# A router product with its weight columns stationary and the tokens streamed

## The chip, the cores and the metric

The kernel runs on one core of one Trainium2 chip. The metric is the device time of one execution, in microseconds (us), lower is better. The times are those of whole executions; the profile is of one execution of its own.

## The reference

One decoder layer in float32: 1024 tokens of width 1024. A mixer (a gated convolution, and stick-breaking attention in 8 heads) is followed by the output projection and the residual sum, and then by a hierarchical mixture of experts. The change is about the router, the first lines of `hierarchical_moe`:

```
xf = rms_norm(x)                               # 1024 tokens x 1024
g_logits = xf @ w_group  + b_group             # 4 columns
e_logits = xf @ w_expert + b_expert            # 32 columns
g_idx = argmax(g_logits)                       # one of 4 groups per token
e_in_group = e_logits.reshape(N, 4, 8)[g_idx]  # its 8 experts
top_v, top_i = top_k(e_in_group, 2)            # two experts per token
```

Each token is then multiplied with the three weight matrices of its two experts, weighed by its gates and added to the residual.

## The kernel before, in words

The kernel is a row of blocks with a barrier of all engines between them: projections, attention and convolution; then the block at line 807, in which the change lies; then the choice of experts (line 1032); then the loop over the 32 experts, the blocks that didn't fit, and the sum.

The block at line 807 goes over eight tiles of 128 tokens, m = 0 to 7. TensorE has an order written out by hand (lines 862 to 885). `multiply(m, h, ...)` forms one half (512 columns) of the output projection of a tile in 24 products: fp32 is split into a high and a low part, both fp32r, and three products (lines 840 to 842) of stationary 128x128 and streamed 128x512 make one of the eight steps. VectorE adds the residual (`add`, line 934), ScalarE squares and sums (909, 911), and VectorE scales the row with the norm (936, 938). TensorE turns the normalised tile in eight transposes (`turn`, line 851), ScalarE copies it out as `xn2T` (line 901), and TensorE forms the router logits of that tile (`route`, line 859). VectorE adds the bias (`bias`, line 942). GpSimd and VectorE prepare the high and low parts of the next tiles (832, 922).

TensorE's queue for tile m is: the first half of the projection of m, `turn(m - 1)`, the second half of m, `route(m - 1)`. VectorE's queue is `add(m)`, the low part of tile m + 2, `bias(m - 1)`. After the loop come `turn(7)`, `route(7)` and `bias(7)`, and then the barrier.

The router product of a tile is eight products of plain fp32, each of which the chip runs as two passes (16 weight loads and 16 matmuls). The stationary operand is the turned tile (128 rows by 128 tokens) and the streamed one `router_w[:, k]` (36 columns); the result is `ps[:, 6 + m % 2, 0:36]`, tokens on partitions. `router_b` holds the bias broadcast to all 128 partitions; it is loaded in two transfers (lines 323, 324) in the first block, on SyncE's queue between loads of x tiles (line 308).

Other lines that are spoken of: 407 is the input projection (128x128 stationary, 512 streamed, fp32r). In attention, 443 to 445 are the scores (64 rows by 128 columns stationary), 446 adds the mask (128x128), 456 transposes, and 466 multiplies with the values (128 rows by 64 columns stationary, 128 streamed, plain fp32).

Of the kernel before, what the change touches and what calls it, by code (L numbers as in the profile page):

```python
# [19 lines left out]
ALU = mybir.AluOpType  # L20
# [3 lines left out]
P = 128  # L24
# [19 lines left out]
def hymba_moe_layer(nc, x, norm_mix_w, w_in, conv_w, q_norm_w, k_norm_w, group_norm_conv_w,  # L44
# [3 lines left out]
    KT = D // P  # L48
    NT = S // P
# [6 lines left out]
    NG = w_group.shape[2]  # L56
# [7 lines left out]
    LOG = NG + NE  # L64
# [13 lines left out]
    with ExitStack() as ctx:  # L78
# [70 lines left out]
        def keep(name, shape, dt=F32):  # L149
            size = 4  # L150
            for n in shape[1:]:
                size *= n
            kib = small[0] / KIB
            small[0] += (size + 31) // 32 * 32
            assert small[0] <= ROOM
            return at(name, kib, shape, dt)
# [15 lines left out]
        q_minus = [keep(f"q_minus{i}", [P, NT, 2]) for i in range(2)]  # L172
        q_log = keep("q_log", [P, NT, 2])
        router_w = keep("router_w", [P, KT, LOG])
        router_b = keep("router_b", [P, LOG])
        logits = keep("logits", [P, NT, LOG])

        def start_step(pool):
# [107 lines left out]
        with nc.Block(no_gpsimd_drain=True) as block:  # L286

            @block.sync
            def _(sp):
                sp.dma_start(xt[0], xv[0]).then_inc(x_landed[0], 16)  # L290
                for i in range(4):
                    sp.dma_start(wv_raw[:, 2 * i:2 * i + 2], w_in_v[:, 2 * i:2 * i + 2, W_IN_BLOCK["v"] * CW:]).then_inc(wv_landed[i], 16)
                    if i == 0:
                        sp.dma_start(g1b, norm_mix_w.partition_broadcast(P)[:, 0, :]).then_inc(g1_in, 16)
                        sp.dma_start(xt[1], xv[1]).then_inc(x_landed[1], 16)

                def load_chunk(c):
                    kind, j = CHUNKS[c]
                    cols = slice(W_IN_BLOCK[kind] * CW + j * P, W_IN_BLOCK[kind] * CW + (j + 1) * P)
                    if c >= 2:  # L300
                        sp.wait_ge(filled, 2 * (c - 1))
                    sp.dma_start(w_raw[c % 2], w_in_v[:, :, cols]).then_inc(w_landed[c % 2], 16)

                load_chunk(0)
                load_chunk(1)
                for m in range(2, NT):
                    sp.wait_ge(x_scaled, m - 1)
                    sp.dma_start(xt[m % 2], xv[m]).then_inc(x_landed[m % 2], 16)
                    if m == 2:
                        for h in range(2):  # L310
                            rows = slice(h * HD, (h + 1) * HD)
                            sp.dma_start(q_gain[rows], q_norm_w.rearrange("a d -> d a")).then_inc(consts_in, 16)
                            sp.dma_start(k_gain[rows], k_norm_w.rearrange("a d -> d a")).then_inc(consts_in, 16)
                        with nc.allow_non_contiguous_dma(reason="small columns"):
                            sp.dma_start(gain_conv, group_norm_conv_w.rearrange("a (b g) d -> (g d) (a b)", g=2)).then_inc(consts_in, 16)
                            sp.dma_start(gain_attn, group_norm_attn_w.rearrange("a (b g) d -> (g d) (a b)", g=2)).then_inc(consts_in, 16)
                            for j in range(TAPS):
                                sp.dma_start(taps[:, j, :], conv_w[0, j].rearrange("(b p) -> p b", p=P)).then_inc(consts_in, 16)
                    if m == 5:
                        with nc.allow_non_contiguous_dma(reason="small columns"):  # L320
                            sp.dma_start(router_w[:, :, 0:NG], w_group.rearrange("a (p k) g -> p (a k) g", k=KT)).then_inc(router_in, 16)
                            sp.dma_start(router_w[:, :, NG:], w_expert.rearrange("a (p k) g -> p (a k) g", k=KT)).then_inc(router_in, 16)
                        sp.dma_start(router_b[:, 0:NG], b_group.partition_broadcast(P)[:, 0, :]).then_inc(router_in, 16)
                        sp.dma_start(router_b[:, NG:], b_expert.partition_broadcast(P)[:, 0, :]).then_inc(router_in, 16)
                for c in range(2, len(CHUNKS)):
                    load_chunk(c)
                sp.wait_ge(filled, 2 * len(CHUNKS))
                for j in range(CB):
                    sp.dma_start(w_out_raw[:, 2 * j:2 * j + 2], w_out_v[:, 2 * j:2 * j + 2]).then_inc(w_out_in[j], 16)
                sp.wait_ge(router_in, 16 * 4)  # L330
# [468 lines left out]
        xn2_turned = sem("xn2_turned")  # L799
        xn2T_made = sem("xn2T_made")  # L800
        logits_summed = sem("logits_summed")
        logits_made = sem("logits_made")
        xn2_stored = [sem(f"xn2_stored{i}") for i in range(2)]
        xn2_rows_v = xn2_rows.rearrange("(m p) d -> m p d", p=P)
# [2 lines left out]
        with nc.Block(no_gpsimd_drain=True) as block:  # L807
# [26 lines left out]
            @block.tensor  # L834
            def _(pe):
                def multiply(m, h, chunks):
                    o = ps[:, 2 * (m % 2) + h]
                    cols = slice(h * BANK, (h + 1) * BANK)
                    for c in chunks:
                        pe.matmul(o, yT_hi[m % 2][:, c], w_out_hi[:, c, cols], start=(c == 0), stop=False)  # L840
                        pe.matmul(o, yT_hi[m % 2][:, c], w_out_lo[:, c, cols], start=False, stop=False)
                        mm = pe.matmul(o, yT_lo[m % 2][:, c], w_out_hi[:, c, cols], start=False, stop=(c == LAST))
                    if c == LAST:
                        mm.then_inc(mixed, 1)

                def turn(m):
                    pe.wait_ge(xn2_made, m + 1)
                    if m:
                        pe.wait_ge(xn2T_made, m)
                    for k in range(KT):  # L850
                        mm = pe.transpose(psf[:, 4 * BANK + k * P:4 * BANK + (k + 1) * P], xn2[m % 2][:, k:D:KT], ident)
                    mm.then_inc(xn2_turned, 1)

                def route(m):
                    pe.wait_ge(xn2T_made, m + 1)
                    if m >= 2:
                        pe.wait_ge(logits_made, m - 1)
                    for k in range(KT):
                        mm = pe.matmul(ps[:, 6 + m % 2, 0:LOG], xn2T[m % 2][:, k], router_w[:, k], start=(k == 0), stop=(k == KT - 1))
                    mm.then_inc(logits_summed, 1)  # L860

                pe.wait_ge(y_lo_made, 1)
                for c in range(LAST):
                    if c == 3:
                        pe.wait_ge(s_n2["squared"], 1)
                        for h in range(2):
                            pe.matmul(ps[:, 4 + h], same_head, last_sq[:, h * BANK:(h + 1) * BANK], start=True, stop=True).then_inc(s_n2["summed"], 1)
                    pe.wait_ge(w_out_lo_made, c + 1)
                    for h in range(2):
                        multiply(0, h, (c,))  # L870
                pe.wait_ge(w_out_lo_made, LAST + 1)
                pe.wait_ge(y_lo_made, 3)
                for h in range(2):
                    multiply(0, h, (LAST,))
                for m in range(1, NT):
                    pe.wait_ge(y_lo_made, m + 3 if m >= 2 else 4)
                    for h in range(2):
                        if h:
                            turn(m - 1)
                        if m >= 2:  # L880
                            pe.wait_ge(x2_made, 2 * m + h - 3)
                        multiply(m, h, range(2 * CB))
                    route(m - 1)
                turn(NT - 1)
                route(NT - 1)

            @block.scalar
            def _(act):
# [31 lines left out]
            def _(dve):  # L920
                def y_lo(m, rows):
                    dve.tensor_tensor(yT_lo[m % 2][:, rows], y_mix[:, rows, m * P:(m + 1) * P], yT_hi[m % 2][:, rows].bitcast(F32),
                                      ALU.subtract).then_inc(y_lo_made, 1)
# [15 lines left out]

                def bias(m):  # L940
                    dve.wait_ge(logits_summed, m + 1)
                    dve.tensor_tensor(logits[:, m], ps[:, 6 + m % 2, 0:LOG], router_b, ALU.add).then_inc(logits_made, 1)

                w_out_rest(0)
                dve.wait_ge(y_hi_made, 1)
# [14 lines left out]
                for m in range(NT):  # L960
                    add(m)
                    if m + 2 < NT:
                        dve.wait_ge(y_hi_made, m + 5)
                        y_lo(m + 2, slice(0, 2 * CB))
                    if m:
                        bias(m - 1)
                bias(NT - 1)

        room = [128 * KIB]

# [602 lines left out]
```

## Time and profile before

| | |
|---|---|
| median of 3 runs | 1360.22 us (1358.24 to 1361.03) |
| the profiled execution | 1359.96 us, its span 1358.3 us |
| mean granted TensorE clock | 0.939 |
| TensorE busy | 1207.4 us, 89% of the span |
| VectorE busy | 870.9 us, 64% |
| ScalarE busy | 732.0 us, 54% |
| GpSimd busy | 147.1 us, 11% |

The span runs from the first to the last instruction; the device time is 1.66 us longer. PE is the matmul side of TensorE and PEld its weight loads, which overlap the matmuls. DVE is VectorE, ACT ScalarE, POOL GpSimd, SP SyncE. The granted clock 1.00 is 2.4 GHz, 0.50 is 1.2 GHz. Because matmuls are pipelined, a busy TensorE is not one at its peak: what a matmul costs in a dense stretch is the distance from its start to the next one's start, not its duration. "issue" as the end of a pause means that nothing the profile shows was waited for.

### The profile page before, as it was taken

How to read it: one execution, taken by the hardware profiler on the slowest of the kernel's cores; microseconds unless marked ns; L12 is line 12 of the kernel's file. 1: busy time of each engine (PE TensorE's matmuls, PEld its weight loads, DVE VectorE, ACT ScalarE, POOL GpSimd, SP SyncE). 2: the span in 40 equal slices, each digit the busy share in tenths (PEclk: the TensorE clock that was granted, in tenths of full speed). 3: DMA queues.
4: the chain of work that ended last, by engine and by line, in shares of the span. 5: the costliest groups of instructions: out<-in, count | busy, mean ns of one | idle time of the engine just before them, and what ended most of it. 6: DMA issues, size and time to landing. Idle time of an engine off the chain costs nothing. (4 is left out here: it accounts for less than half of the span.)

```text
span 1358.3 us, 16775 instructions
## 1 busy us (share of the span) xinstructions
PE 1207.4 (89%) x5870; PEld 977.8 (72%) x5870; DVE 870.9 (64%) x910; ACT 732.0 (54%) x918; POOL 147.1 (11%) x194
## 2 busy tenths in 40 slices
PE   5999989979988997699945999999999999999930
PEld 4887767757767776488834888888888888888830
DVE  4414444434426454543264999999999999999926
ACT  4322433543453243521104788888888888888820
POOL 1000000000010003010002011111111111111000
PEclk9999979989999998799957999999999999999975
DMA  6111100100000103331064899999999999999509
GB/s 199 39 31 32 32 16 16 32 15 16 16 16 16 32 16 124 147 148 47 31 263 154 322 379 384 382 384 387 380 384 384 381 383 385 389 381 378 204 17 371
DMA packets 57339, 261.89 MB, mean 193 GB/s; under 512 B 13008, under 2 KB 33488, under 8 KB 43984
## 3 DMA queue, kind: packets, MB, share of 16 engines
q1 hardware_dynamic: 46928, 240.31, 46.3%
q0 software_dynamic: 9216, 16.80, 3.3%
q10 hardware_dynamic: 1152, 4.19, 0.8%
q8 instruction: 29, 0.48, 0.1%
q14 instruction: 14, 0.11, 0.0%
HBM read 252.88 MB, written 25.17 MB: 205 GB/s over the span
## 5 line engine op out<-in xcount | busy, mean ns | idle before, releaser
L1245 DVE TENSOR_TENSOR e_lo<-W,e_hi 128x1024 fp32r<-128x1024 f32 x384 | 452.7, 1221 | 25.0 <-ACT e_hi L1239 21.9
L1239 ACT ACTIVATE e_hi<-W 128x1024 fp32r<-128x1024 f32 x384 | 403.3, 1060 | 96.3 <-PE ps L1210 96.3
L730 DVE TENSOR_TENSOR_SCAN kept<-kept 128x128 f32<-128x128 f32 (+7 forms) x64 | 90.3, 1410 | 222.9 <-ACT kept L587 190.1
L1208 PE MATMUL ps<-e_hi,xT_hi 128*128 128x512 f32 x512 | 204.3, 399 | 7.1 <-DVE e_lo L1245 7.1
L1210 PE MATMUL ps<-e_lo,xT_hi 128*128 128x512 f32 x512 | 201.6, 394 | 0.0
L1209 PE MATMUL ps<-e_hi,xT_lo 128*128 128x512 f32 x512 | 200.9, 392 | 0.0
L586 ACT ACTIVATE soft<-ps,q_scale 128x128 f32<-128x128 f32 (+7 forms) x54 | 38.0, 704 | 194.2 <-PE ps L456 183.0
L407 PE MATMUL ps<-xnT_hi,w_hi 128*128 128x512 f32 x320 | 129.2, 404 | 12.6 <-DVE u L698 6.0
L407 PE MATMUL ps<-xnT_lo,w_hi 128*128 128x512 f32 x320 | 129.2, 404 | 0.0
L407 PE MATMUL ps<-xnT_hi,w_lo 128*128 128x512 f32 x320 | 129.2, 404 | 0.0
L1208 PEld LDWEIGHTS ps<-e_hi,xT_hi 128*128 128x128 f32 x512 | 97.6, 191 | 26.8 <-issue 4.0
L1210 PEld LDWEIGHTS ps<-e_lo,xT_hi 128*128 128x128 f32 x512 | 96.9, 189 | 20.8
L1209 PEld LDWEIGHTS ps<-e_hi,xT_lo 128*128 128x128 f32 x512 | 97.3, 190 | 19.3
L1208 PE MATMUL ps<-e_hi,hidT_hi 128*128 128x512 f32 x256 | 102.5, 401 | 2.7 <-DVE e_lo L1245 2.7
L466 PE MATMUL ps<-probsT,v 128*64 128x128 f32 x576 | 83.3, 294 | 19.1 <-ACT probsT L601 19.1
L1210 PE MATMUL ps<-e_lo,hidT_hi 128*128 128x512 f32 x256 | 100.1, 391 | 0.0
L1209 PE MATMUL ps<-e_hi,hidT_lo 128*128 128x512 f32 x256 | 100.0, 391 | 0.0
L466 PEld LDWEIGHTS ps<-probsT,v 128*64 128x64 f32 x576 | 67.1, 146 | 42.6 <-ACT probsT L601 26.8
L1302 POOL DMA_INDIRECT y_rows<-y,idx_pair x32 | 32.6, 1019 | 457.1 <-ACT y L1265 457.1
L407 PEld LDWEIGHTS ps<-xnT_hi,w_hi 128*128 128x128 f32 x320 | 61.2, 191 | 26.2 <-issue 14.6
L407 PEld LDWEIGHTS ps<-xnT_lo,w_hi 128*128 128x128 f32 x320 | 61.8, 193 | 11.9 <-issue 0.2
L407 PEld LDWEIGHTS ps<-xnT_hi,w_lo 128*128 128x128 f32 x320 | 61.7, 193 | 11.8
(211 smaller groups left out, 1801.2 us busy)
## 6 DMA issues: line engine op xcount, KB each, us to landing
W<-in_w_dram SPq DMA_DIRECT2D x96, 2048.0 KB, 10.1
w_raw<-in_w_in_dram SPq DMA_DIRECT2D x20, 512.0 KB, 4.0
yy<-y_rows SPq DMA_DIRECT2D x8, 1024.0 KB, 13.5
xt<-in_x_dram SPq DMA_DIRECT2D x8, 512.0 KB, 3.5
w_out_raw<-in_w_out_dram SPq DMA_DIRECT2D x4, 1024.0 KB, 8.4
xn_rows<-xn SPq DMA_DIRECT2D x8, 512.0 KB, 2.6
out_dram<-x ACTq DMA_DIRECT2D x8, 512.0 KB, 8.9
x<-in_x_dram SPq DMA_DIRECT2D x1, 3072.0 KB, 13.5
```

The lines of the kernel that those rows point to most:

```text
L407: mm = pe.matmul(ps[:, 6 + g % 2], w, r, start=(i % TICKS == 0), stop=(i % TICKS == TICKS - 1))
L466: mm = pe.matmul(ps[h * HD:(h + 1) * HD, VB, (t % 4) * P:(t % 4 + 1) * P], v[:, j, head], probsT[:, j, :], start=(j == 0), stop=(j == t))
L586: act.activation(soft[n % 2][:, 0:length(n)], z, ACT.Sigmoid, scale=up)
L730: dve.tensor_tensor_scan(back, back, back, 1.0, ALU.mult, ALU.min).then_inc(multiplied, 1)
L1208: pe.matmul(o, xs_hi[:, k], e_hi[:, p, cols], start=(k == 0), stop=False)
L1209: pe.matmul(o, xs_lo[:, k], e_hi[:, p, cols], start=False, stop=False)
L1210: mm = pe.matmul(o, xs_hi[:, k], e_lo[:, p, cols], start=False, stop=(k == last))
L1239: act.activation(e_hi[:, p], flat[:, p * D:(p + 1) * D], ACT.Copy).then_inc(s["hi_made"], 1)
L1245: dve.tensor_tensor(e_lo[:, p], flat[:, p * D:(p + 1) * D], e_hi[:, p], ALU.subtract).then_inc(s["lo_made"], 1)
L1302: pool.indirect_dma_start(out=y_rows, out_offset=bass.IndirectOffsetOnAxis(ap=idx_pair[b].bitcast(U32), axis=0), in_=y[b], in_offset=None, ...
```

## The change

The operands of the router product change places: `router_w[:, k]` (36 columns) is stationary and the turned tile (128 tokens) is streamed, so that the result has the 36 logits on partitions and the tokens along the row, in bank 6. The bias is then one value per partition, loaded as a column, and VectorE adds it while it copies the result to a new tile `logits_T`. TensorE turns this 36x128 tile back in one transpose (`turn_logits`, into bank 7), and VectorE copies the 36 columns of the tile to `logits` (`take_logits`). Each of the two new steps has a place of its own in the queues: `turn_logits(m - 2)` behind the first half of the projection of tile m, `take_logits(m - 2)` ahead of `bias(m - 1)`.

```diff
-        router_b = keep("router_b", [P, LOG])
+        router_b = keep("router_b", [LOG, 1])
+        logits_T = [keep(f"logits_T{i}", [LOG, P]) for i in range(2)]
...
-                        sp.dma_start(router_b[:, 0:NG], b_group.partition_broadcast(P)[:, 0, :]).then_inc(router_in, 16)
-                        sp.dma_start(router_b[:, NG:], b_expert.partition_broadcast(P)[:, 0, :]).then_inc(router_in, 16)
+                        sp.dma_start(router_b[0:NG], b_group.rearrange("a g -> g a")).then_inc(router_in, 16)
+                        sp.dma_start(router_b[NG:], b_expert.rearrange("a g -> g a")).then_inc(router_in, 16)
...
                 def route(m):
                     pe.wait_ge(xn2T_made, m + 1)
                     if m >= 2:
+                        pe.wait_ge(logits_biased, m - 1)
+                    for k in range(KT):
+                        mm = pe.matmul(ps[0:LOG, 6, m % 2 * P:(m % 2 + 1) * P], router_w[:, k], xn2T[m % 2][:, k], start=(k == 0), stop=(k == KT - 1))
+                    mm.then_inc(logits_summed, 1)
+
+                def turn_logits(m):
+                    pe.wait_ge(logits_biased, m + 1)
+                    if m >= 2:
                         pe.wait_ge(logits_made, m - 1)
-                    for k in range(KT):
-                        mm = pe.matmul(ps[:, 6 + m % 2, 0:LOG], xn2T[m % 2][:, k], router_w[:, k], start=(k == 0), stop=(k == KT - 1))
-                    mm.then_inc(logits_summed, 1)
+                    pe.transpose(ps[:, 7, m % 2 * P:m % 2 * P + LOG], logits_T[m % 2], ident[0:LOG, 0:LOG]).then_inc(logits_turned, 1)
...
                         multiply(m, h, range(2 * CB))
+                        if h == 0 and m >= 2:
+                            turn_logits(m - 2)
                     route(m - 1)
                 turn(NT - 1)
+                turn_logits(NT - 2)
                 route(NT - 1)
+                turn_logits(NT - 1)
...
                 def bias(m):
                     dve.wait_ge(logits_summed, m + 1)
-                    dve.tensor_tensor(logits[:, m], ps[:, 6 + m % 2, 0:LOG], router_b, ALU.add).then_inc(logits_made, 1)
+                    if m >= 2:
+                        dve.wait_ge(logits_turned, m - 1)
+                    dve.tensor_scalar(logits_T[m % 2], ps[0:LOG, 6, m % 2 * P:(m % 2 + 1) * P], router_b, None, ALU.add).then_inc(logits_biased, 1)
+
+                def take_logits(m):
+                    dve.wait_ge(logits_turned, m + 1)
+                    dve.tensor_copy(logits[:, m], ps[:, 7, m % 2 * P:m % 2 * P + LOG]).then_inc(logits_made, 1)
...
+                    if m >= 2:
+                        take_logits(m - 2)
                     if m:
                         bias(m - 1)
+                take_logits(NT - 2)
                 bias(NT - 1)
+                take_logits(NT - 1)
```

## Rows read from the trace of the kernel before

**Rows 1.** Waits in 582 to 688 us: who for whom: total us, times, longest

```profile
DVE x L934 <- PE ps L842: 55.1, 14, 5.7
PE ps L851 <- DVE xn L938: 2.1, 1, 2.1
PE ps L859 <- ACT xn2T L901: 1.1, 1, 1.1
```

**Rows 2.** Stretches: length, busy us of each engine (instructions), granted clock, DMA share, GB/s

```profile
609.00:663.00 54.00, 54.00 (x286) 46.21 (x285) 15.78 (x24) 9.88 (x16) 3.46 (x4) 1.00 0.10 40
...
681.30:732.50 51.20, 20.34 (x97) 14.48 (x97) 29.57 (x97) 8.61 (x10) 6.97 (x15) 0.50 0.48 189
...
746.00:749.60 3.60, 3.60 (x10) 2.78 (x10) 3.17 (x4) 2.10 (x3) 0.00 (x0) 0.53 0.13 52
750.00:1309.00 559.00, 553.26 (x2614) 463.59 (x2612) 526.81 (x497) 459.01 (x464) 83.33 (x119) 1.00 0.92 358
```

**Rows 3.** TensorE in order of time, tile 2: start us, us, instruction, tiles, shapes, count

```profile
612.65 0.39 PE L840 MATMUL ps<-w_out_hi,yT_hi 128*128 128x512 f32 x1
...
615.14 0.40 PE L842 MATMUL ps<-w_out_hi,yT_lo 128*128 128x512 f32 x1
615.38 1.04 PE L851 MATMUL ps<-ident,xn 128*128 128x128 f32 x8
...
616.49 0.39 PE L841 MATMUL ps<-w_out_lo,yT_hi 128*128 128x512 f32 x1
...
621.50 0.39 PE L842 MATMUL ps<-w_out_hi,yT_lo 128*128 128x512 f32 x1
621.73 1.87 PE L859 MATMUL ps<-router_w,xn2T 128*128 128x36 f32 x16
...
623.75 0.39 PE L841 MATMUL ps<-w_out_lo,yT_hi 128*128 128x512 f32 x1
```

**Rows 4.** TensorE in order of time, value products between projection and scores

```profile
442.79 1.96 PE L466 MATMUL ps<-probsT,v 128*64 128x128 f32 x16
...
477.59 0.39 PE L407 MATMUL ps<-xnT_hi,w_lo 128*128 128x512 f32 x1
477.91 0.63 PEld L466 LDWEIGHTS ps<-probsT,v 128*64 128x64 f32 x6 [0.35 <-issue]
477.91 0.87 PE L466 MATMUL ps<-probsT,v 128*64 128x128 f32 x6
...
479.05 0.39 PE L444 MATMUL ps<-k_lo,q_hi 64*128 64x512 f32 x1
```

**Rows 5.** TensorE in order of time, ends of a short group of scores

```profile
116.25 0.39 PE L407 MATMUL ps<-xnT_hi,w_lo 128*128 128x512 f32 x1
...
118.23 0.40 PE L407 MATMUL ps<-xnT_lo,w_hi 128*128 128x512 f32 x1
```

**Rows 6.** Waits of the weight loads, 100 to 560 us

```profile
PEld ps L466 <- issue: 15.8, 43, 0.7
...
PEld ps L446 <- issue: 10.4, 32, 0.4
```

**Rows 7.** All engines in order of time, end of the block

```profile
682.50 3.63 PE L859 MATMUL ps<-router_w,xn2T 128*128 128x36 f32 x16 [1.11 <-ACT xn2T L901]
686.17 0.20 DVE L942 TENSOR_TENSOR logits<-ps,router_b 128x36 f32<-128x36 f32 x1 [5.89 <-PE ps L859]
...
686.73 0.33 SPq L1036 DMA_DIRECT2D W<-in_w_dram  x1
```

**Rows 8.** VectorE in order of time, tile 2

```profile
613.07 0.19 DVE L942 TENSOR_TENSOR logits<-ps,router_b 128x36 f32<-128x36 f32 x1
```

**Rows 9.** Single lines: count, duration ns min/median/max, first and last start, forms

```profile
L859 PE MATMUL ps<-router_w,xn2T x128: 193/279/430, 594.5 to 685.7; 128*128 128x36 f32 x128
...
L1276 DVE CAST hidT_hi<-ps x32: 683/684/692, 755.4 to 1297.6; 128x512 fp32r<-128x512 f32 x32
```

**Rows 10.** SyncE's queue in order of time, bias loads and the next x tile

```profile
33.04 2.50 SPq L323 DMA_DIRECT2D router_b<-in_b_group_dram  x1
...
38.12 6.69 SPq L308 DMA_DIRECT2D xt<-in_x_dram  x2
```

More of the change, by code:

```diff
@@ L801, in hymba_moe_layer @@
         logits_summed = sem("logits_summed")
+        logits_biased = sem("logits_biased")
+        logits_turned = sem("logits_turned")
         logits_made = sem("logits_made")
```

## The prediction, made before the changed kernel was run

> **What bounds the kernel now.** I read the waits of the output projection stage first, then the stretches by engine, then the order of time around one token tile. In the stage from about 584 to 686 us everybody waits for TensorE: VectorE stands before its residual add until the product is done, 14 times and 55.1 us in all [rows 1]. TensorE itself stops only at the end: 2.1 us ahead of the last token transposes and 1.1 us ahead of the last router product [rows 1]. Between 609 and 663 us it is busy all 54.00 us at full granted clock, VectorE 15.78 of them [rows 2]. So here each nanosecond that is added to TensorE's queue, or taken out of it, is one of the span. Behind the stage comes a barrier, and the next expert weights (line 1036) are asked for only at 686.73 [rows 7]; from 750 to 1309 us TensorE is busy 553 of 559 us [rows 2]. A shift of the barrier goes through to the end.
>
> **The router product, 16 passes per tile, by stream length alone.** The ordinary cadence of the 128x512 products is 0.226 us: 612.65 to 615.14 are 11 steps in 2.49 us [rows 3]. From the last product ahead of the router (621.50) to the second one behind it (623.75) are 2.25 us, less two cadences 1.80 us, so 0.112 us a pass [rows 3]. The eight token transposes, which stream 128 columns and not 36, come to 616.49 - 615.14 - 0.45 = 0.90 us, also 0.112 each [rows 3]: today 128 stationary columns are loaded per pass, and the load hides the short stream. After the change 36 columns are loaded and 128 streamed. The nearest rows are the value products of line 466 (64 stationary columns, 128 streamed, fp32, two passes each as here): 16 of them take 1.96 us and 6 take 0.87 us, so (1.96 - 0.87)/10 = 0.109 us a pass [rows 4]. Loading less buys nothing, since the stream takes the load's place: 16 x 0.109 = 1.74 us against 1.80.
>
> **The array's shape, a cost the diff doesn't name.** Line 466 has stationary operands of 128x64 and its neighbours 128x128. In its row the weight load doesn't start with the product before it, as loads of equal shape do, but late, with 0.35 us of idle that is put down to "issue", to nothing that the profile shows [rows 4]. This happens 43 times at line 466 and 32 times at line 446, where the shape goes from 64 rows back to 128 [rows 6]. The price: from 477.59 (line 407) to 479.05 (second product of the scores) are 1.46 us; two cadences and 6 passes would be 0.45 + 0.65 = 1.11, so 0.35 us for the pair of changes, in and out [rows 4]. For the 64x128 shape: from 116.25 to 118.23 are 1.98 us, with eight short products between (lines 443, 444, 445 with 64 rows, then 446 with 128, twice over), so four changes; without them 0.45 + 8 x 0.109 = 1.32, and the rest is 0.66, or 0.16 us a change [rows 5].
> The Trainium skill, TensorEngine Tiling (Array Packing), Key Properties, says that changing the tiling mode, not just the tile, drains TensorE; it lists 128x64 and 64x128 as modes beside 128x128. By that rule the trace's late loads are such drains, the trace agrees, and a 36-wide operand would be one too; the page has no price.
> Now the router product has 128x36 operands, and the small transposes back have logits_T as stationary operand, 36 rows by 128. I take both as narrower shapes that pay as these two rows do. Bounds for one change: nothing, if 36 counts as full width; 0.09 us, if only the lateness of the load counts (477.59 to 477.91, less a cadence [rows 4]); and 0.2 us from above (half of 0.35, and a little for the wider load on the way out). Between them I take the rows' own whole prices.
> Router product: 1.74 + 0.35 = 2.09 against 1.80, +0.29 us. Small transpose: one pass 0.11 + two changes of 0.16 = +0.43 us. It sits ahead of turn(m - 1), between full-width products, so it pays both changes and shares none with the router product.
> How many lie on the path: turn_logits(0) to (5) stand inside m = 2 to 7, ahead of the last large product, and route(0) to (5) too. 6 x (0.29 + 0.43) = 4.3 us. Bounds: 6 x (0.12 + 0.29) = 2.5 where a change costs 0.09, 6 x (-0.06 + 0.11) = 0.3 where it costs nothing, 6 x (0.34 + 0.51) = 5.1 at 0.2. route(6) gets longer inside the 2.1 us in which TensorE waits for the last normalised tile. turn_logits(6) lies in the 1.1 us gap ahead of route(7) [rows 1]: 0.43 us, or 0.87 at half clock, fit. If these covers were gone they would cost 0.3 and 0.9 us.
>
> **The new waits.** turn_logits(m) waits for the bias of its tile, with the token transposes and half of the large product queued behind it. VectorE adds the bias at 613.07 [rows 8] and TensorE comes by only at 615.38 [rows 3]. VectorE now does two things there, take_logits and bias. Its time from PSUM is 0.19 us for 36 elements [rows 8] and 0.684 for 512 [rows 9], so by a straight line 0.285 for the 128 of the turned bias: both done at about 613.55, 1.8 us early. take_logits(m - 2) waits for a transpose that was issued ahead of turn(m - 1), long before. +0.28 us a tile on VectorE, which has waits of 55.1 us to spare: cost nothing; if TensorE did meet it, it would cost what is beyond 1.8 us.
>
> **The tail, all on the path.** At the end of the last router product VectorE adds and the barrier comes; now it adds, TensorE turns once more, VectorE copies. The last product runs at granted clock 0.50 [rows 2], which is 1.2 of 2.4 GHz, (3.63 - 0.41)/15 = 0.215 us a pass [rows 7], twice the full-clock price whether load or stream sets it, so nothing changes in it. Added: bias 0.285 instead of 0.20 (+0.08), handing over twice (+0.06 and +0.04, as 686.13 to 686.17 [rows 7]), one pass on an empty array, up to 0.43 us (the longest of line 859 [rows 9]), and the copy 0.19: +0.80 us. From 0.6 (a pass of 0.28) to 1.1 (a second pass length of load ahead of it). The drain is hidden here by the wait for the bias.
>
> **The bias loads.** Two broadcasts of 128 rows become two column loads with 36 small pieces, on the same place of SyncE's queue. The first held the queue from 33.04 for 2.50 us; the next load, at 38.12, waits for VectorE anyway [rows 10]. If they hold the queue for less, it is free sooner for nobody; even if each took 2.5 us, they would end at 38.04. Nothing either way.
>
> **Sum.** 4.3 + 0.8 = +5.1 us on the profiled execution's own 1359.96 us (span 1358.3 and 1.66 around it), which is 0.26 below the median of the runs: 1365.1 us.
>
> **The rivals.**
> Shapes cost nothing (36 of 128 treated as full width): 6 x 0.05 + 0.8 = +1.1 us, 1361.1, no measurable change. For it: no row shows an operand 36 wide, the narrow ones are 64. Against: no row of a narrower shape at full clock is free of the late load. It decides from a price below about 0.08 us a change (24 changes at 0.08 and 1.1 are 3.0). Chance 0.09.
> The streamed pass is short: a row for 128 columns at half the price, 0.055 us. Then 6 x 16 x 0.057 = 5.5 us and 16 x 0.107 = 1.7 in the tail come off against 6 x 0.11 + 0.8 without changes of shape: 1354.2 us, faster. If shapes do cost, 6 x (0.35 + 0.32) of it is given back: 1358.2. Against it are the 0.109 us of line 466. The Trainium skill, TensorE: Matmul & The Clock Gate, Back-to-back issue gap, gives N/2.4 + 2.5 ns, 55.8 ns for 128 columns, as an estimate the price of this rival; the trace has twice that for an fp32 pass. Chance 0.04.
> The clock: TensorE is at half clock from 681.3 to 732.5 us [rows 2], after pauses of 2.1 and 1.1 us [rows 1], in both kernels. If it rose 3.6 us later (746.00 to 749.60 is such a stretch, granted 0.53 [rows 2]), that would cost half of it, 1.8 us; as much the other way. 1366.9, or 1363.3. For it speaks that the runs differ by up to 2.8 us, against it that the pauses stay as they are. Chance of the slower 0.07, of the other 0.05.
> TensorE meets VectorE at turn_logits: it needs 1.8 us more per tile on VectorE, against a computed 0.28. At 1 us a tile, 1371. Chance 0.02.
>
> **How the numbers follow.** My forecast with its own terms 0.73, the rivals as given. The likeliest case by its bounds: 2.5 + 0.6 to 5.1 + 1.1, 1363.1 to 1366.2; runs of the same kernel lie up to 2.8 us apart. With the clock's cases the range becomes 1362.2 to 1367.6. About 0.2% (2.7 us) is what a measurement of this kernel can tell from no change. Slower by more than that, above 1362.9: 0.82. Within it: 0.13, of it 0.09 the free shapes and 0.04 a cheap change of shape. Faster: 0.05.
>
> **What the profile after would show.** A projection stage that is longer by about 4.3 us up to its last 128x512 product, with VectorE's wait for line 842 longer by as much. The router's first weight load about 0.09 us after the end of the stream before it, and not with its start, and the same at the small transpose and behind both: "issue" idle on the load queue, four times a tile. Router passes at 0.109 us. The barrier some 0.8 us later behind the last router product. Wrong would be: loads on time around 36-wide shapes, passes at half of 0.109, a TensorE wait for the bias, or an unchanged stage with the loss elsewhere.

## The result, and the profile after

| | before | after |
|---|---|---|
| median of 8 runs each, taken together | 1361.32 us (1358.24 to 1362.70) | 1367.78 us (1361.90 to 1369.63) |
| profiled execution: time, span | 1359.96, 1358.3 us | 1364.81, 1363.1 us |
| mean granted clock of it | 0.939 | 0.942 |

The ratio is 1.0041 with an interval of 1.0030 to 1.0051: slower by 5.6 us, 4.1 to 6.9 (the two medians alone are 6.5 us apart). Forecast were +5.1 us and 1365.1 us on a base of 1360.22; the interval of the loss holds the forecast one, while the new median itself, with a base that also came out 1.1 us higher here, lies 0.2 us above the range that was given.

The waits of the same stretch as [rows 1], changed kernel: who for whom, total us, times, longest:

```profile
DVE x L947 <- PE ps L845: 57.8, 14, 6.1
...
PEld ps L862 <- issue: 2.5, 7, 0.4
PEld ps L869 <- issue: 2.4, 7, 0.4
...
PE ps L854 <- DVE xn L951: 1.9, 1, 1.9
...
PEld ps L843 <- issue: 1.2, 6, 0.2
...
PE ps L862 <- ACT xn2T L914: 0.9, 1, 0.9
```

The changed kernel's output projection in two stretches, up to its last 128x512 product and from there to the next block's first VectorE work (columns as in [rows 2]). The first is counted from the start of the last product with `same_head` (line 867 before, 876 here), which stands among the large products of tile 0:

```profile
575.14:680.50 105.36, 105.04 (x526) 84.80 (x524) 33.19 (x51) 20.81 (x32) 8.54 (x8) 1.00 0.20 82
680.50:693.74 13.24, 7.85 (x44) 5.78 (x42) 3.23 (x8) 3.75 (x5) 1.35 (x7) 0.69 0.18 54
```

The reader is to see three things. TensorE is still busy in 105.04 of 105.36 us, and VectorE's wait for it has grown by 2.7 us from the 55.1 of [rows 1]: the stage is bound as it was. Three lines now have idle that is put down to "issue" in every tile; none of them stands in [rows 1]. And no TensorE wait for the bias is there but the one at the very end.

The same two stretches of the kernel before are 101.22 and 12.25 us. So the profiles differ by +0.33 us ahead of the stage, +4.13 in it, +0.99 in the tail and -0.62 behind it, +4.84 in all. The parts outside hold no instruction that the change concerns but the bias loads; the stretches at granted clock 0.5 lie a little elsewhere in each execution (289.5 to 296.3 and 299.8 to 310.0 us after, 292.2 to 309.2 before). Over all nine profiles of this document the part ahead of the stage ends between 573.3 and 576.3 us.

One token tile of the changed kernel, TensorE in order of time, where [rows 3] stood before:

```profile
616.47 0.39 PE L845 MATMUL ps<-w_out_hi,yT_lo 128*128 128x512 f32 x1
616.79 0.25 PE L869 MATMUL ps<-ident,logits_T 36*128 36x36 f32 x1
616.97 1.16 PE L854 MATMUL ps<-ident,xn 128*128 128x128 f32 x8
...
618.21 0.39 PE L844 MATMUL ps<-w_out_lo,yT_hi 128*128 128x512 f32 x1
...
623.22 0.39 PE L845 MATMUL ps<-w_out_hi,yT_lo 128*128 128x512 f32 x1
623.53 1.94 PE L862 MATMUL ps<-xn2T,router_w 128*36 128x128 f32 x16
...
625.74 0.40 PE L844 MATMUL ps<-w_out_lo,yT_hi 128*128 128x512 f32 x1
```

And the weight loads of those moments:

```profile
616.79 0.14 PEld L869 LDWEIGHTS ps<-ident,logits_T 36*128 36x128 f32 x1 [0.35 <-issue]
...
623.53 1.67 PEld L862 LDWEIGHTS ps<-xn2T,router_w 128*36 128x36 f32 x16 [0.35 <-issue]
625.40 0.19 PEld L843 LDWEIGHTS ps<-w_out_hi,yT_hi 128*128 128x128 f32 x1 [0.20 <-issue]
```

By the prediction's own arithmetic: from the last product ahead of the router (623.22) to the second one behind it (625.74) are 2.52 us, less two cadences 2.07, against 1.80 before. From 616.47 to 618.21 are 1.74, less two cadences 1.29, against 0.90 for the token transposes alone. The router's first load starts 0.31 us after the start of the product ahead of it, whose stream takes 0.226; loads between operands of equal width start together with that product. That is the late load, at 36 columns and at 36 rows as at 64. The prediction named four such loads a tile; three have idle put down to "issue". The fourth change, from the small transpose back to the token transposes, shows as 0.18 us from start to start (616.79 to 616.97) where a pass takes 0.11.

### The profile page after: what moved, and what is told of

It is laid out like the page before. It is cut to its first block and busy times, and to the rows that moved or that the text cites. A ratio compares the mean times of both kernels' runs of the same rounds, so it can differ in the third digit from the quotient of the medians.

```text
span 1363.1 us, 16811 instructions
## 1 busy us (share of the span) xinstructions
PE 1208.4 (89%) x5878; PEld 973.1 (71%) x5878; DVE 875.3 (64%) x918; ACT 732.5 (54%) x918; POOL 143.4 (11%) x194
```

## The experiments

Five of the kernels have one run each, so for them the trace carries the verdict: the length of one tile (the same VectorE add, one tile apart, equal in tiles 2 to 7) and the stage up to its last large product, both in us. "Tail" is what follows up to the next block's first VectorE work. Beside adjacent and the two dummy kernels the kernel before had one run of its own, 1360.2 us. The single time of pad_route is short because the part ahead of its stage ends 1.5 us earlier than in the kernel before (573.3 and 574.8 us), ahead of all products that its edit concerns. The diffs are shortened: `slot` and `...` stand for indices that stay, and memsets of the padding and the waits for them, ahead of the stage, are not shown.

| kernel | one tile | stage | tail | time |
|---|---|---|---|---|
| before | 13.63 | 101.2 | 12.25 | 1361.3, median |
| after | 14.32 | 105.4 | 13.24 | 1367.8, 8 runs |
| pad_both | 13.77 | 102.1 | 13.97 | 1364.6, 8 runs |
| pad_route | 14.03 | 103.6 | 12.85 | 1361.8, one run |
| pad_turn | 14.07 | 103.8 | 12.75 | 1364.6, one run |
| adjacent | 14.07 | 103.7 | 12.75 | 1364.6, one run |
| twin_groups | 13.27 | 99.1 | 12.36 | 1359.1, 11 runs |
| dummy_full | 14.59 | 108.0 | 12.24 | 1367.5, one run |
| dummy_narrow | 15.53 | 114.6 | 12.25 | 1374.4, one run |

**pad_both: the changed kernel with both narrow operands made full width.** The slice of 36 weight columns is read on into the ones behind it (128 in all; the surplus results are ignored), and logits_T gets 128 rows, of which 92 are zero.

```diff
-mm = pe.matmul(ps[0:LOG, 6, slot], router_w[:, k], xn2T[m % 2][:, k], ...)
+mm = pe.matmul(ps[:, 6, slot], router_flat[:, k*LOG:k*LOG+P], xn2T[m % 2][:, k], ...)
-pe.transpose(ps[:, 7, m%2*P:m%2*P+LOG], logits_T[m%2], ident[0:LOG, 0:LOG])
+pe.transpose(ps[:, 7, m%2*P:(m%2+1)*P], logits_T[m%2], ident)
```

> The changed kernel with both new operands widened to the full array: the router's stationary slice takes 128 columns (its 36 and what lies behind them), and logits_T is a 128x128 tile whose rows 36 to 127 are zero, turned whole. Every instruction and wait of the changed kernel stays; only the shapes differ. Theory (changes of the array's shape cost, 24 of them on the path): the stage up to the last 128x512 product falls back to 6 x (-0.03 + 0.11) = about +0.5 us over the kernel before, from +4.1; with the tail +1.3 in all, 1362.6 us against 1361.3, ratio 1.001. The weight loads start with the product before them. Rival (the added transpose, its waits and the streamed passes cost by themselves): the stage stays at +4.1 and the ratio at 1.004.

Measured: 1364.57 us (1363.49 to 1367.64, 8 runs) against 1361.35, ratio 1.0025 (1.0014 to 1.0036). TensorE of this kernel in order of time, then the load, then the same VectorE add one tile apart:

```profile
616.46 0.39 PE L850 MATMUL ps<-w_out_hi,yT_lo 128*128 128x512 f32 x1
616.69 0.27 PE L874 MATMUL ps<-ident,logits_T 128*128 128x128 f32 x1
```

```profile
616.47 0.14 PEld L874 LDWEIGHTS ps<-ident,logits_T 128*128 128x128 f32 x1
```

```profile
623.39 0.69 DVE L953 TENSOR_TENSOR x<-ps,x 128x512 f32<-128x512 f32 x1 [5.80 <-PE ps L850]
...
637.16 0.69 DVE L953 TENSOR_TENSOR x<-ps,x 128x512 f32<-128x512 f32 x1 [5.81 <-PE ps L850]
```

The load starts 0.01 us behind the start of the large product ahead of it, no "issue" idle is left at lines 867 and 874, and a tile takes 13.77 us, 0.14 more than before the change instead of 0.69. Same instructions and hand-overs, wider operands: 0.55 of the 0.69 us is the width, and 0.14 is left for the added transpose, whose pass alone is 0.11. The stage is +0.9 us, where +0.5 was expected.

The time is a miss: +3.2 us where +1.3 was expected, and the ratio expected, 1.001, lies outside the interval. The stage (+0.9) and the longer chain behind the last router product (+0.77, in the profile) explain 1.65 us of it; the other 1.6 us have no shown cause. The profiled execution took 1367.16 us, 2.6 above the median. Its tail is 1.72 us longer than before: beside the chain's 0.77, the granted clock fell at 682.4 us, at the start of the last token transposes, so that they took 1.95 us instead of 1.16 and the router product 3.78 instead of 3.63. A second fall, near the end, is told in the last section.

**pad_route and pad_turn: one of the two edits each.**

> Only the router's stationary slice widened to 128 columns, the small transpose 36x128 as in the changed kernel. Theory: the router product costs 0.03 less than before per tile, the turn 0.43 more: the stage is +2.4 us over the kernel before (changed kernel +4.1). If the router's shape cost nothing, it stays at +4.1.

> Only logits_T widened to 128 rows and turned whole, the router's stationary slice 36 columns as in the changed kernel. Theory: the turn costs 0.11 per tile, the router product +0.29: the stage is +2.4 us over the kernel before (changed kernel +4.1). If the transpose's shape cost nothing, it stays at +4.1.

The same VectorE add in three successive halves, first with the router's operand full, then with logits_T full:

```profile
621.24 0.69 DVE L951 TENSOR_TENSOR x<-ps,x 128x512 f32<-128x512 f32 x1 [6.07 <-PE ps L848]
...
628.51 0.69 DVE L951 TENSOR_TENSOR x<-ps,x 128x512 f32<-128x512 f32 x1 [2.06 <-PE ps L848]
...
635.27 0.69 DVE L951 TENSOR_TENSOR x<-ps,x 128x512 f32<-128x512 f32 x1 [6.07 <-PE ps L848]
```

```profile
624.34 0.69 DVE L951 TENSOR_TENSOR x<-ps,x 128x512 f32<-128x512 f32 x1 [5.80 <-PE ps L848]
...
631.92 0.69 DVE L951 TENSOR_TENSOR x<-ps,x 128x512 f32<-128x512 f32 x1 [2.37 <-PE ps L848]
...
638.41 0.69 DVE L951 TENSOR_TENSOR x<-ps,x 128x512 f32<-128x512 f32 x1 [5.80 <-PE ps L848]
```

Measured: 14.03 and 14.07 us a tile, +0.40 and +0.44 where +0.4 was expected, and stages 2.4 and 2.6 us longer than before. With the router's operand full the router half of a tile is 7.27 us as before (7.28), and the half with the small transpose 6.76 (6.35 before); with logits_T full they are 7.58 and 6.49 (0.14 above before, as in the padded kernel). The two parts add up to the whole: 0.29 for the router product, 0.40 for the small transpose, of which 0.14 stays when its operand is full.

**dummy_full and dummy_narrow: the price of a change of shape by itself.** The kernel before, with 28 small products put between large ones of half 0 (their outputs go to a bank that the next half overwrites); the two differ in the width of the stationary operand and of the result alone. In both, TensorE's wait `x2_made` ahead of half 0 is the one that stood ahead of half 1, because of that bank; TensorE shows no wait for it in either profile.

```diff
+if m and h == 0 and c in (0, 2, 4, 6):
+    pe.matmul(ps[:, 2*(m%2)+1, 0:64], ident, ident[:, 0:64], ...)            # dummy_full
+    pe.matmul(ps[0:64, 2*(m%2)+1, 0:64], ident[:, 0:64], ident[:, 0:64], ...) # dummy_narrow
...
-                            pe.wait_ge(x2_made, 2 * m + h - 3)
+                            pe.wait_ge(x2_made, 2 * m - 2)
```

> The kernel before, with four fp32 products added in the first half of each tile 1 to 7, their results unused: stationary 128x128, 64 columns streamed, two passes each, put between the full-width products of the projection. Control for the next run: 2 x 0.112 = 0.22 us each by both theories, 0.9 us a tile.

> The same four products per tile with a stationary operand of 128x64, half the columns to load. Theory (a change of shape waits for the end of the stream and about 0.09 us, and then shows its whole weight load): late 0.09 + load 0.055 + two passes 0.11 + late 0.09 + load of the next 0.11 = 0.45 us each, 1.8 us a tile, twice the full-width control though it loads less. Rival (only instructions and bytes cost): 0.11 to 0.22 us each, not above the control.

TensorE around one of them, first full width, then 64 columns:

```profile
616.52 0.40 PE L842 MATMUL ps<-w_out_hi,yT_lo 128*128 128x512 f32 x1
616.76 0.33 PE L844 MATMUL ps<-ident 128*128 128x64 f32 x2
616.90 0.48 PE L840 MATMUL ps<-w_out_hi,yT_hi 128*128 128x512 f32 x1
617.21 0.39 PE L841 MATMUL ps<-w_out_lo,yT_hi 128*128 128x512 f32 x1
```

```profile
617.29 0.40 PE L842 MATMUL ps<-w_out_hi,yT_lo 128*128 128x512 f32 x1
617.62 0.33 PE L844 MATMUL ps<-ident 128*64 128x64 f32 x2
617.87 0.50 PE L840 MATMUL ps<-w_out_hi,yT_hi 128*128 128x512 f32 x1
618.21 0.40 PE L841 MATMUL ps<-w_out_lo,yT_hi 128*128 128x512 f32 x1
```

From line 842 to line 841 are 0.69 and 0.92 us; less two cadences a small product costs 0.24 us at full width and 0.47 at half, though it loads half as much. A tile has four: +0.96 and +1.90 us on 13.63, against 0.88 and 1.80 expected. A pair of changes is 0.23 us dearer than the very same product without them.

**adjacent: the small transpose moved beside the router product.** Instructions as in the changed kernel, in another order: three changes of shape a tile instead of four. `route` waits for the bias of the tile before; TensorE never stops for it.

```diff
-                    if m >= 2:
-                        pe.wait_ge(logits_biased, m - 1)
+                    if m:
+                        pe.wait_ge(logits_biased, m)
...
-                        if h == 0 and m >= 2:
-                            turn_logits(m - 2)
                     route(m - 1)
+                    if m >= 2:
+                        turn_logits(m - 2)
```

> The changed kernel with turn_logits(m - 2) moved behind route(m - 1), so that the 128x36 and the 36x128 operands follow each other: three changes of shape a tile in place of four, the same instructions (route waits in addition for the bias of the tile before). Theory: a tile takes 0.20 us less than in the changed kernel, 14.12 us against 14.32. Rival (cost by instruction or by narrow operand): 14.32 as before.

```profile
623.88 1.94 PE L862 MATMUL ps<-xn2T,router_w 128*36 128x128 f32 x16
625.75 0.25 PE L869 MATMUL ps<-ident,logits_T 36*128 36x36 f32 x1
625.93 0.50 PE L843 MATMUL ps<-w_out_hi,yT_hi 128*128 128x512 f32 x1
```

Measured: 14.07 us a tile, 0.25 less than 14.32, where 14.12 was expected. The two narrow products stand together (625.75), and full width is back at 625.93. Order alone gives back a third of the loss. Beside the router product the small transpose costs 0.15 us a tile with its pass of 0.11, between large products 0.40. Its load is late here too (625.75, with 0.20 us of idle put down to "issue"), so the step from 36 columns to 36 rows counts as a change, but a cheap one: 0.04 us by this sum, less than the 0.12 to 0.18 of the others.

**twin_groups: the two halves of the array's columns at once.** Even chunks of the contraction go to columns 0 to 35, odd ones to columns 64 to 99; the product that turns the logits back adds the two; it is now a plain fp32 product of two passes with a stationary operand of 100 rows.

```diff
+at_row = 64 * (k % 2)
-mm = pe.matmul(ps[0:LOG, 6, slot], router_w[:, k], xn2T[m%2][:, k], start=(k == 0), ...)
+mm = pe.matmul(ps[at_row:at_row+LOG, 6, slot], router_w[:, k], xn2T[m%2][:, k], start=(k < 2), ...)
-pe.transpose(ps[:, 7, slot], logits_T[m%2], ident[0:LOG, 0:LOG])
+pe.matmul(ps[:, 7, slot], logits_T[m%2][0:64+LOG], both[0:64+LOG], ...)   # both: two identities stacked
```

> The changed kernel with the router product split over two column halves of the array: even k into partitions 0 to 35, odd k into 64 to 99 of the same bank, and the turn back as one product with a 100x36 matrix that adds the two halves (two fp32 passes, full width). If two streams can run at once in the two halves, a router product takes 0.13 + 8 x 0.109 + 0.20 = 1.2 us in place of 2.1, the turn 0.22 without changes of shape, and the last router product at half clock 1.7 us less: 6 x (1.2 - 1.8 + 0.22) - 1.7 + 1.0 = about -2.9 us against the kernel before, ratio 0.998. If the streams follow one another: 6 x (0.29 + 0.22) + 1.0 = +4.1 us, ratio 1.003.

```profile
622.23 0.39 PE L850 MATMUL ps<-w_out_hi,yT_lo 128*128 128x512 f32 x1
622.55 1.07 PE L868 MATMUL ps<-xn2T,router_w 128*36 128x128 f32 x16
...
623.89 0.40 PE L849 MATMUL ps<-w_out_lo,yT_hi 128*128 128x512 f32 x1
```

Measured: 1359.06 us (1356.05 to 1362.68, 11 runs), ratio 0.9983 (0.9973 to 0.9993): 2.3 us faster than the kernel before and the fastest of all. The 16 passes take 1.07 us where they took 1.94, with both changes still paid; a tile is 13.27 us, 0.36 under before (0.38 expected), the stage 2.2 us shorter. In all 2.9 us were expected. What is missing is in the tail, where 0.7 us less was expected and the profile has 0.1 more: the last router product is 1.70 us shorter and the chain behind it 1.09 longer, but the granted clock fell at 679.3 us, ahead of the last token transposes, and they took 1.97 us instead of 1.16.

## Why the prediction was right, step by step

**The bound.** What was put into TensorE's order of a tile, or taken out of it, showed up in the tile's length in each of the eight edited kernels. VectorE, which [rows 1] has waiting, waited longer in the changed one, but by 2.7 us and not by the stage's 4.1 as the prediction said: its own work in the stage grew from 31.80 to 33.19 us, and that fills the rest.

**Router product, +0.29 forecast.** The half of a tile with it went from 7.28 to 7.57 us: +0.29. Between changes the passes take 0.109 us each, as [rows 4] had for 64 columns, against 0.112 with 128 columns loaded, and so loading 36 gained what the prediction gave it, some 0.05 us a tile. The rival of the short pass falls.

**Change of shape.** Free shapes (rival, 1361.1 us) fall with pad_both and with the dummies. The Trainium skill, TensorEngine Tiling (Array Packing), Key Properties, says that a change of mode drains TensorE. The trace agrees with a drain as far as the late load shows one (0.31 us instead of about nothing), and the runs put a price on it: 0.23 us for a pair beyond a small product of full width, 0.35 for the pair around the router product.

**Small transpose, +0.43 forecast, +0.40 measured.** 6.35 to 6.75 us. Its two changes came to 0.15 each instead of 0.16. Together 0.69 a tile against 0.72, and the stage +4.13 against +4.3.

**Bias and waits, nothing forecast.** VectorE's copy of tile 0's logits and bias of tile 1's in the changed kernel ([rows 8] is the same bias before; its heading says tile 2, the tile whose projection is being formed is 3):

```profile
614.10 0.19 DVE L961 COPY logits<-ps 128x36 f32<-128x36 f32 x1
614.20 0.33 DVE L957 TENSOR_SCALAR logits_T<-ps,router_b 36x128 f32<-36x128 f32 x1
```

The bias is done at 614.53 and TensorE asks for it at 616.79: 2.3 us early where 1.8 were forecast, although it takes 0.33 us and not 0.285. The rival in which TensorE meets VectorE falls.

**Tail, +0.80 forecast, +0.99 measured.** All engines at the end of the block, changed kernel, beside [rows 7]:

```profile
684.70 1.40 PE L854 MATMUL ps<-ident,xn 128*128 128x128 f32 x8 [1.94 <-DVE xn L951]
...
687.21 3.63 PE L862 MATMUL ps<-xn2T,router_w 128*36 128x128 f32 x16 [0.86 <-ACT xn2T L914]
690.87 0.34 DVE L957 TENSOR_SCALAR logits_T<-ps,router_b 36x128 f32<-36x128 f32 x1 [4.30 <-PE ps L862]
691.27 0.32 PE L869 MATMUL ps<-ident,logits_T 36*128 36x36 f32 x1 [0.43 <-DVE logits_T L957]
691.63 0.20 DVE L961 COPY logits<-ps 128x36 f32<-128x36 f32 x1 [0.41 <-PE ps L869]
```

The router product takes 3.63 us as before. Behind its end (690.84) VectorE was done after 0.99 us, against 0.24 in [rows 7]: +0.75, from a pass of 0.32 (up to 0.43 was priced), a bias of 0.34 and a copy of 0.20. The other 0.24 us are the token transposes ahead of it, 1.40 us instead of 1.16: in this execution the granted clock (third number from the end of this row of stretches) is at half from 685.5, in the middle of them, and in the one before from 681.3 [rows 2], behind them.

```profile
681.00:685.00 4.00, 2.06 (x18) 1.79 (x17) 2.42 (x5) 1.44 (x3) 0.00 (x0) 1.00 0.00 0
685.50:736.70 51.20, 20.14 (x99) 13.30 (x98) 29.69 (x98) 7.64 (x10) 6.99 (x15) 0.50 0.48 189
```

They are the clock's and not the edit's: in the adjacent kernel, whose clock fell at 686.0, those transposes take 1.16 and the same last router product 3.45.

**The clock's rivals, 1366.9 and 1363.3 us.** Neither came in the profiled executions: the half-clock stretch is 51.2 us long before and after, and the later one 3.4 us. The prediction puts the fall behind both pauses [rows 1]; it lies at 681.3 us, ahead of the second, which ends at 682.50 [rows 7].

**Bias loads, nothing forecast.** SyncE's queue in the changed kernel, beside [rows 10]:

```profile
31.81 1.13 SPq L324 DMA_DIRECT2D router_b<-in_b_group_dram  x1
32.98 1.20 SPq L325 DMA_DIRECT2D router_b<-in_b_expert_dram  x1
36.88 0.35 SPq L309 DMA_DIRECT2D xt<-in_x_dram  x1
```

They hold the queue for 1.13 and 1.20 us, the next x load again waits for VectorE, and when the projection stage begins the two kernels are 0.33 us apart.

**The sum.** Stage and tail together went from 113.47 to 118.60 us: +5.13, forecast +5.1. The terms' errors (-0.17 in the stage, -0.05 in the chain, +0.24 by the clock, for which the sum had no term) cancel, which is luck; the stage and the chain alone are 0.22 us under the forecast. The interval of the timed difference, 4.1 to 6.9 us, holds it.

**What stays open.** The timed medians lie 6.5 us apart and the ratio says 5.6, the profile's path 5.1; in the padded kernel 1.6 us are unexplained in the same direction. The runs of the changed kernel spread over 7.7 us, those of the kernel before over 4.5. Each run's mean granted clock was noted: it was 0.936 to 0.939 in the changed kernel's five runs above 1367 us, 0.942 in the two at 1364.3 and 1364.8, and 0.940 in the fastest, 1361.9. Of 18 runs of the kernel before, taken beside the padded kernel, 14 had 0.941 or more. So a lower clock was the more frequent one in the changed kernel's runs, but no trace of one of its longer runs was kept, and neither the stretch that lost it nor a link to the edit is shown.

## What to carry to other kernels

On a TensorE that is the bound, count the changes of array shape in its order as instructions of their own: about 0.12 to 0.18 us each here at full clock between narrow and full width, whichever side is narrow, and put narrow products side by side so that they share them (0.25 us a tile here). Making a narrow operand stationary and streaming the wide one bought some 0.05 us a tile here, where a pass went from 0.112 to 0.109 us; it begins to pay when the free columns do work at the same time, as in the two column groups.

## What was not expected of the hardware

Two products in the two halves of the array's columns run truly beside one another, fp32 and with separate loads: 16 passes in 1.07 us, 8 pairs at 0.109 and the end of the last. The product that turns the logits back there has a stationary operand of 100 rows. Its load starts with the large product ahead of it (615.67), without "issue":

```profile
615.68 0.42 PEld L875 LDWEIGHTS ps<-both,logits_T 100*128 100x128 f32 x2
```

So 100 of 128 rows behave as full width here, 36 rows as narrow, and so do the 64 rows of the scores, whose first load in the kernel before starts 0.31 us behind the start of the product ahead of it (116.56 and 116.25). Where between 64 and 100 the line lies was not measured.

Near the end of the expert loop TensorE waits 2.7 us for VectorE in every kernel. In two of nine profiles the granted clock goes to half in the last microsecond of that wait. The padded kernel, TensorE's first product behind the wait, and the stretch around it:

```profile
1304.40 0.76 PE L1238 MATMUL ps<-e_hi,hidT_hi 128*128 128x512 f32 x1 [2.73 <-DVE e_lo L1275]
```

```profile
1303.60:1310.50 6.90, 6.10 (x15) 4.79 (x15) 4.07 (x4) 0.00 (x0) 1.39 (x2) 0.51 0.10 39
```

and the changed kernel, the same product and stretch:

```profile
1304.99 0.47 PE L1231 MATMUL ps<-e_hi,hidT_hi 128*128 128x512 f32 x1 [2.73 <-DVE e_lo L1268]
```

```profile
1303.60:1310.50 6.90, 5.51 (x24) 4.43 (x24) 4.65 (x5) 0.20 (x1) 1.39 (x2) 1.00 0.10 39
```

The same pause to 0.01 us, once with 15 products at 1.2 GHz behind it, once with 24 at 2.4. The expert loop takes 586.3 us in the first and 582.3 in the second, and 585.3 with the two column groups, where the half-clock stretch is 1300.6 to 1304.0; the seven others are within 582.3 to 583.2. So the same instructions can differ by some 3 us from execution to execution. It is part of why the padded kernel's profiled execution is long; whether its other runs, 2.6 us lower by the median, had the fall too is not known. Single times in the table above are therefore read behind the traces.
